# Expert weights of a mixture of experts: `down` in four neighbouring rows to a partition, every fourth inner column to a column tile, and three strips for the first two blocks

## What is computed

```
pg = softmax(xt @ w_group + b_group);  g_prob, g_idx = top_k(pg, 1)          # 4 groups
le = (xt @ w_expert + b_expert) of the chosen group; e_prob, e_local = top_k(softmax(le), 2)
...
ys = (silu(xb @ w_gate[e]) * (xb @ w_up[e])) @ w_down[e]      # each token's two experts
out = sum over its two experts of gate * ys
```

## Time and profile before

| | |
|---|---|
| median of three runs | 4483.69 us (4479.28 to 4484.81) |
| profiled execution | 4486.34 us, span 4484.4 us |
| granted TensorE clock over the span | 0.958 |
| TensorE matmul busy | 4098.7 us, 91% |
| VectorE, ScalarE, GpSimd busy | 45%, 25%, 11% |
| DMA | 285125 packets, 710.31 MB |
| TensorE L2593, all 192 strips of both layers | 208.7 + 204.9 + 151.2 + 147.7 us busy |

### The profile page before, as it was taken

The page is one execution under the profiler, slowest core; times in us unless marked ns, Lnnn a source line. Parts: engine busy times, 40 slices in busy tenths (PEclk is TensorE's granted clock), DMA queues, the critical chain, the costliest instruction groups (busy, mean ns, idle before and its releaser), DMA issues. The chain is left out here.

```text
span 4484.4 us, 83646 instructions
## 1 busy us (share of the span) xinstructions
PE 4098.7 (91%) x36682; PEld 2459.4 (55%) x36682; DVE 2013.2 (45%) x2980; ACT 1109.2 (25%) x1919; POOL 509.0 (11%) x348
## 2 busy tenths in 40 slices
PE   7999999899999998999896999976999998899993
PEld 3555664445556645665454556543666664555652
DVE  4565356455545554555553111106657776111114
ACT  2333223134432221222200000003444530000003
POOL 1232011032211100000000000000312200000001
PEclk9999999999999999999897999987999998899996
DMA  3323202232320244445324999982000122799996
GB/s 103 113 95 104 61 24 90 72 109 90 109 82 28 85 160 84 76 79 90 78 82 170 394 393 401 403 327 80 15 2 14 39 82 85 265 399 400 403 395 257
DMA packets 285125, 710.31 MB, mean 158 GB/s; under 512 B 57307, under 2 KB 184739, under 8 KB 267735
## 3 DMA queue, kind: packets, MB, share of 16 engines
q1 hardware_dynamic: 271751, 658.70, 42.3%
q0 software_dynamic: 11808, 41.95, 2.8%
q10 hardware_dynamic: 1200, 4.24, 0.2%
HBM read 631.82 MB, written 64.60 MB: 155 GB/s over the span
## 5 line engine op out<-in xcount | busy, mean ns | idle before, releaser
L493 PE MATMUL ps<-sb_xT,sb_work 128*128 128x512 f32 x768 | 359.9, 605 | 9.6 <-ACT sb_x_tok L846 5.5
L493 PE MATMUL ps<-sb_mixT,sb_work 128*128 128x512 f32 x768 | 359.5, 604 | 9.6 <-ACT sb_x_tok L846 5.5
L1632 PE MATMUL ps<-sb_xT,sb_work 128*128 128x512 f32 x512 | 236.2, 600 | 0.0
L2593 PE MATMUL ps<-sb_work,sb_mixT 128*32 128x256 f32 x3584 | 208.7, 388 | 12.4 <-DMA sb_work<-moe_w_up 11.7
L493 PEld LDWEIGHTS ps<-sb_xT,sb_work 128*128 128x128 f32 x768 | 138.0, 192 | 148.1 <-issue 130.1
L493 PEld LDWEIGHTS ps<-sb_mixT,sb_work 128*128 128x128 f32 x768 | 138.0, 192 | 147.8 <-issue 129.9
L2593 PE MATMUL ps<-sb_work,sb_xT 128*32 128x256 f32 x3584 | 204.9, 383 | 6.7 <-DMA sb_work<-moe_w_up 5.9
L2108 DVE TENSOR_REDUCE sb_cols<-ps 128x1 f32<-128x1024 f32 x128 | 150.6, 1218 | 85.8 <-PE ps L1951 85.7
L2677 DVE TENSOR_TENSOR sb_work<-ps,sb_work 128x512 f32<-128x512 f32 (+2 forms) x66 | 61.6, 933 | 260.2 <-PE ps L2616 260.2
L2660 ACT COPY sb_work<-ps 128x256 f32<-128x256 f32 (+2 forms) x66 | 31.0, 470 | 591.6 <-PE ps L2604 591.6
L2593 PEld LDWEIGHTS ps<-sb_work,sb_mixT 128*32 128x32 f32 x3584 | 117.1, 112 | 92.0 <-issue 22.7
(11 more groups left out here) (486 smaller groups left out, 7268.4 us busy)
## 6 DMA issues: line engine op xcount, KB each, us to landing
sb_work<-moe_w_gate SPq DMA_DIRECT2D x34, 2048.0 KB, 8.2
sb_work<-moe_w_up SPq DMA_DIRECT2D x34, 2048.0 KB, 12.6
sb_work<-moe_w_down SPq DMA_DIRECT2D x32, 2048.0 KB, 21.3
sb_mixT<-moe_w_down SPq DMA_DIRECT2D x17, 2048.0 KB, 22.2
sb_xT<-moe_w_down SPq DMA_DIRECT2D x17, 2048.0 KB, 22.0
sb_xT<-moe_w_gate SPq DMA_DIRECT2D x16, 2048.0 KB, 16.0
sb_xT<-moe_w_up SPq DMA_DIRECT2D x16, 2048.0 KB, 22.1
sb_mixT<-moe_w_gate SPq DMA_DIRECT2D x16, 2048.0 KB, 15.9
```

The source lines that it names most:

```text
L493: last = pe.matmul(m.ps[:, bank, :], b.w[i][:, k, :], m.xT[:, k, half * HALF:(half + 1) * HALF], start=(k == 0), stop=(k == NK - 1))
L1632: last = pe.matmul(m.ps[:, bank, :], w[j // 2][:, k, :], m.xT[:, k, j % 2 * HALF:(j % 2 + 1) * HALF], start=(k == 0), stop=(k == NK - 1))
L2593: last = pe.matmul(strip_sums(2 + 2 * (n % 2), tile[j])[:, g, :], b.x_turned[n % 2][:, k, g * STRIP:(g + 1) * STRIP], b.gate_up[n % 2][:, ...
```

## The change

Four edits belong together, and a fifth is separate.

1. Down is loaded by `by_rows`: partition p holds the rows 4p to 4p+3, 16 KB in one piece. This holds for the 33 loads of each layer and for the overflow loop.
2. For this the inner columns must be grouped otherwise. Column tile j now takes the inner columns 4c+j instead of 128j+c; the moving operand of `product` steps by four elements, 16 bytes, in gate and in up. All else in `turn_h` and `down` stays as it was.
3. Blocks 0 and 1 have three strips instead of four, 94 strips in all. The order of blocks changes with it: 3 fourteen times, then 4 2 seven times over, and 2 2 2 2 2: the last wide block is followed by six narrow ones.
4. `skip_places` has one more operation on VectorE.
5. `clear_overflow` clears two more pieces, rows 96 to 127 of blocks 0 and 1.

```diff
-    places = [(b, rows_of(b)) for b in range(WIDE_BLOCKS, N_EXPERTS)] + [(b, 0) for b in range(N_FIXED, N_BLOCKS)]
+    places = [(b, rows_of(b)) for b in range(N_EXPERTS) if rows_of(b) < P] + [(b, 0) for b in range(N_FIXED, N_BLOCKS)]
...
 def strips_of(block):
-    return 4 - (block >= WIDE_BLOCKS) - (block >= MIDDLE_BLOCKS) if block < N_EXPERTS else 4
+    if block >= N_EXPERTS:
+        return 4
+    return 4 - (block < N_FIRST) - (block >= WIDE_BLOCKS) - (block >= MIDDLE_BLOCKS)
...
-    order, strips = list(range(N_FIRST)), 4 * N_FIRST
+    order, strips = list(range(N_FIRST)), 3 * N_FIRST
...
-            sp.dma_start(experts.down[0], a["moe_w_down_2"][l, 0].rearrange("(k p) n -> p k n", p=P)).then_inc(
+            sp.dma_start(experts.down[0], by_rows(a["moe_w_down_2"][l, 0])).then_inc(
...
             def skip_places(dst, at, n, spare, least):
-                do(dve.tensor_scalar(spare, at, MIDDLE_BLOCKS - 0.5, None, ALU.is_gt))
+                do(dve.tensor_scalar(spare, at, N_FIRST - 0.5, None, ALU.is_lt))
+                do(dve.scalar_tensor_tensor(spare, at, MIDDLE_BLOCKS - 0.5, spare, ALU.is_gt, ALU.add))
...
                     last = pe.matmul(strip_sums(2 + 2 * (n % 2), tile[j])[:, g, :],
                                      b.x_turned[n % 2][:, k, g * STRIP:(g + 1) * STRIP],
-                                     b.gate_up[n % 2][:, :, k, j * P:(j + 1) * P], start=(k == 0), stop=(k == NK - 1))
+                                     b.gate_up[n % 2][:, :, k, :].rearrange("p a (c j) -> p a j c", j=QUARTERS)[:, :, j, :], start=(k == 0), stop=(k == NK - 1))
...
-                sp.dma_start(b.down[n % 2], source(n, "down").rearrange("(k p) n -> p k n", p=P)).then_inc(loads[n % 2][1], 16)
+                sp.dma_start(b.down[n % 2], by_rows(source(n, "down"))).then_inc(loads[n % 2][1], 16)
```

More of the change, by code:

```diff
@@ L2541, in load_expert @@
                      by_rows(a[f"moe_w_{name}_2"][l, bass.ds(expert, 1)].rearrange("a q n -> (a q) n"))).then_inc(semaphores[0], 16)
-    sp.dma_start(buffers.down[n], a["moe_w_down_2"][l, bass.ds(expert, 1)].rearrange("a (k p) n -> p (a k) n", p=P)).then_inc(
+    sp.dma_start(buffers.down[n], by_rows(a["moe_w_down_2"][l, bass.ds(expert, 1)].rearrange("a q n -> (a q) n"))).then_inc(
         semaphores[1], 16)
```

## The result

The changed kernel takes 5121.14 us (median of four runs, 5115.30 to 5125.44), the kernel before in the same session 4481.48 (4474.98 to 4484.81): a ratio of 1.1423, with a 95% interval of 1.1409 to 1.1437. The forecast of 4448 and its range are both wrong. The rival that came true is the halved rate of the product, for which 5103 was worked out. The profiled execution took 5124.02 us, span 5122.2.

What follows compares the result with a forecast made beforehand. DMA was taken to set the pace, TensorE right behind. Per layer 7.2 + 10.2 + 1.0 = 18.4 us; 2 x 18.4 - 0.7 = 36.1 off 4486.3 gives 4450.2, as a median 4448 us; range 4420 to 4550.

Steps and rivals of the forecast that it cites:

- the halved rate of the product: Rival at L2593: 450 ns instead of 225 for 256 elements, 5103 us; chance 0.09 at or above 5103.
- What bounds the kernel: In the expert stages DMA sets the pace by a margin of 3 to 4%, TensorE right behind it.
- So a stream with a step can keep this pace: Product's moving operand: `turn_x`'s 0.85 ns an element against 0.88 needed, so the step was taken to cost nothing.
- 199 against 140 ns: Durations of one load with and without a step, 42% more; named as evidence against a free step in product.
- the bound of 42%: Upper bound on the step's cost in product, of 338 us a layer; with 42% the time is 4711.
- Edit 3, strips: Expert stages: full stretch begins 7.2 us sooner, and fewer stores and gathers save 1.0 us, in each layer.
- the 14.1 foretold: Sign of the earlier start: block 3's loads issued 14.1 us behind block 2's instead of 17.7.
- Its order: Two narrow blocks move from third and fourth to the end; sum of bytes unchanged, no gain counted.
- Edit 1, 16 KB pieces: Loads of down: 0.33 us a load, 31 loads in the full stretch, 10.2 us a layer (bounds 0 and 29).
- down gains nothing: Rival for down's loads: the pieces gain nothing, leaving 7.2 + 1.0 us a layer, 4468 us; chance 0.12.
- The 3 us a layer: Estimate from the skill's fixed packet cost for down's pieces: 1.7%, under 0.1 us a load; forecast 15 us higher.
- Edits 4 and 5: Routing operation costs 4 x 0.18 = 0.7 us; two more clearing transfers, 2.6 us, covered by VectorE's work.

Runs made afterwards that it cites:

- e1: Kernel before plus three strips for blocks 0 and 1, the new order, clearing and routing operation; no step, down in 4 KB pieces: 4457.40 us, ratio 0.9942.
- e2: Changed kernel with the product's moving operand without a step, down still in 16 KB pieces: 4460.88 us, ratio 0.9943 to the kernel before.
- e3: Kernel before with strips as in e1, a step of two elements in product, down in two 8 KB pieces: 4476.05 us, ratio 0.9981.
- e5: Kernel before plus a stage timing matmuls, stationary loads and transposes in groups of 24, with various steps and line patterns: 4775.56 us.
- e7: Kernel before with all of e1 but the order: three strips for the first two blocks in the old order; 4462.72 us, ratio 0.9954.
- e6: Kernel before with the changed order of blocks as the only edit, all blocks keeping their strips: 4474.25 us, ratio 0.9982.
- e4: Kernel before with a stage of matmuls in front, timing single and four-abreast streams and loads with various steps, fp32 and bf16: 4893.62 us.

## Why the prediction was wrong

- **What bounds the kernel.** Right: DMA with a thin margin, and a few per cent on TensorE decide. e1 and e2 keep DMA's share at 1.00 to 1.01; e3's 5% on the product already reaches the total.
- **The step that failed** is in edit 2: "So a stream with a step can keep this pace", from which the cost was taken as nothing. The pace of 0.85 ns an element of `turn_x` was compared with 0.88 ns of the product, two different paths. e5 shows that a transpose's load without a step takes little more than half as long, 1.70 us for 24 against 2.86 with `turn_x`'s step of 8 and 3.06 with a step of 4. The row that was read as a free step was one that had already paid. The other row of the same argument, 199 against 140 ns, pointed the right way and was put second. And the bound of 42% taken from it wasn't a bound: the true cost is 3.78 us on 3.6, 105%. An instruction's duration holds a fixed part beside the streaming, as the 632 and 383 ns show: 65% more in duration, 105% more in pace. The pace is what an engine that is full pays.
- **The rival of the halved rate** had the mechanism and nearly the size: 4483.7 + 676 - 57 = 5103. With 94 x 2 x 3.78 = 711 in place of 676 and less the 11 us estimated for the clock it is 5127, against 5121 measured. The Trainium skill, "Advanced Engine Details and Errata", section "SBUF Cachelines", says that two accesses have to fall in each line of 16 bytes; for fp32 the runs agree (227 ns with two in a line and 217 without a step, 451 with one). For bf16 they do not: two in a line took 227 ns where 113 were had with four, and the measurement decides. With the rule standing in the text and no row of a moving operand against it, 0.09 was too low a chance.
- **Edit 3, strips.** 16 us expected, 20.0 measured (e7), with the start 13.75 to 13.8 us behind block 2's loads instead of the 14.1 foretold. In the changed kernel it is worth 37 by estimate instead, since TensorE is the bound there.
- **Its order.** Taken for nothing, measured at 8.4 us (e6) and 5 (e1 against e7, in two sessions). The cause is open.
- **Edit 1, 16 KB pieces.** Taken for 20 us, none measured (e2 against e1). The rival "down gains nothing" was right in this. The 3 us a layer that the prediction works out from the Trainium skill, "DMA: Bandwidth & Descriptors", can't be told from nothing in these runs; they decide against the 10.2.
- **Edits 4 and 5.** Not tried alone. They are in e1 and e7, whose gains leave no room for a cost of more than a few microseconds.

## What to carry to other kernels

Count the 16-byte lines that a moving operand changes in each partition, not its elements: in these runs 256 fp32 elements take the greater of 216 ns and 1.77 ns a line, so that a layout which makes a DMA prettier by a step in the matmul's operand is paid on TensorE, at full price where every element has a line of its own. When a cost is taken from another instruction, compare it with the same kind of instruction without the feature in question; a pace that looks like the one wanted may already hold the penalty. And price the edit on the engine that runs second before the gain on the one that runs first: here 20 us of a hoped gain stood against 676.

## What the runs showed of the hardware that was not expected

- A step of 2 in fp32 costs 5% (227 against 216 ns for 256 elements), of 3 57% (340), of 4 and more about double (432 to 459). Sharing lines between four streams gives nothing, nor does reading the same 16 lines again.
- The time of a line doesn't follow TensorE's granted clock. In e4 the clock fell while the engine was busy all the time, with the bf16 stream of 16-byte steps, and was at 1.2 GHz in the loads behind it. Windows of e4: bf16 with a step of 8 (with 4, just before, the clock was 1.00), fp32 loads without a step, loads with a step of 8. Behind them the durations and starts of the two kinds of loads.

```profile
339.50:368.00 28.50, 28.50 (x65) 7.82 (x64) 0.00 (x0) 0.00 (x0) 0.00 (x0) 0.57 0.00 0
368.50:395.00 26.50, 26.50 (x127) 26.50 (x126) 0.00 (x0) 0.00 (x0) 0.00 (x0) 0.50 0.00 1
396.00:425.00 29.00, 29.00 (x124) 29.00 (x123) 0.00 (x0) 0.00 (x0) 0.00 (x0) 0.50 0.00 1
```

```profile
L3046 PE MATMUL ps<-sb_x_tok x128: 234/401/402, 368.3 to 395.3; 128*128 128x32 f32 x128
L3048 PE MATMUL ps<-sb_x_tok x128: 402/424/426, 395.5 to 425.7; 128*128 128x32 f32 x128
```

  The bf16 stream at a mean of 0.57 has 452 ns, as the fp32 one at 1.00 has 451. By the distance between starts, loads without a step took 27.0 / 127 = 213 ns at 0.50, against (143.61 - 138.34) / 48 = 110 at 1.00 in e5. Loads with a step of 8 took 30.2 / 127 = 238 ns at 0.50, and (238.94 - 227.72) / 48 = 234 in e5, where the window has a clock of 0.72:

```profile
227.80:238.70 10.90, 10.90 (x48) 10.90 (x48) 0.00 (x0) 0.00 (x0) 0.00 (x0) 0.72 0.00 0
```

  In these rows what is bound by elements slows down with the clock, and what is bound by lines does not.
